# A hybrid decoder trunk on one core: tokens laid out feature by feature, the first norm's squares shared by two engines, router matrix and bias loaded in mid layer

## What is computed

```python
h = jnp.concatenate([meta, x], axis=1)           # 272 x 1024
for layer in range(2):
    u = rmsnorm(h, attn_norm[layer])             # h * rsqrt(mean(h*h) + eps) * gain
    ... = jnp.split(u @ w_in[layer], offsets)    # three token mixers and their gates
    h = h + mixed @ w_out[layer]
    u = rmsnorm(h, ffn_norm[layer])
    # layer 0: dense SwiGLU
    # layer 1: logits = u @ w_router + b_router, the best 2 of 8 experts of each token
return h[:, 16:]
```

## Time and profile before

| what | us |
|---|---|
| median of 3 runs (1881.51 to 1887.78) | 1884.59 |
| the profiled execution, its own time | 1884.42 |
| its span in the trace | 1882.5 |
| PE busy | 1815.8 (96%) |
| DVE busy | 1481.0 (79%) |
| ACT busy | 1284.6 (68%) |
| POOL busy | 111.2 (6%) |
| first product of the first job starts | 21.72 |
| PE idle ahead of the first router logits | 4.08 |

### The profile page before, as it was taken

One profiled execution on the slowest core, in us unless ns is written; L12 is line 12 of the kernel. 1 busy time (PEld: TensorE's weight loads), 2 busy tenths in 40 slices (PEclk: granted clock), 3 DMA queues, 4 the chain that ended last, 5 costly groups with the idle time before them and its releaser, 6 DMA issues.

```text
span 1882.5 us, 29560 instructions
## 1 busy us (share of the span) xinstructions
PE 1815.8 (96%) x10758; PEld 1583.2 (84%) x10758; DVE 1481.0 (79%) x1740; ACT 1284.6 (68%) x1633; POOL 111.2 (6%) x94
## 2 busy tenths in 40 slices
PE   7999999899998998998999999999999999999998
PEld 6988888899997888887888888888888888888886
DVE  5868787655547778777698898988989889898897
ACT  5777676433335776775577777777777777777776
POOL 0000003100010000004300000001000010000101
PEclk9999999999999999999999999999999999999999
DMA  5324324455454333334799999999999999999995
GB/s 196 125 91 133 102 101 141 135 173 177 163 176 149 121 103 112 122 102 152 266 410 370 389 371 371 404 366 391 379 359 406 368 387 369 373 405 369 362 407 214
DMA packets 87108, 485.37 MB, mean 258 GB/s; under 512 B 11630, under 2 KB 11934, under 8 KB 43744
## 3 DMA queue, kind: packets, MB, share of 16 engines
q1 hardware_dynamic: 84080, 476.14, 67.6%
q0 software_dynamic: 2944, 8.09, 1.7%
HBM read 477.17 MB, written 8.41 MB: 258 GB/s over the span
## 4 chain that ended last, share of the span: by engine, by line
PE 80%; DVE 10%; ACT 6%; issue 3%; DMA 1%; POOL 0%; SPq 0%; ACTq 0%; POOLq 0%; DVEq 0%
PE bank L1732 11%; PE bank L1733 11%; PE bank L1737 11%; PE bank L1439 8%; PE bank L1441 8%; PE bank L1440 7%; PE bank L1749 5%; PE bank L1750 5%; PE bank L1755 5%; DVE lo L949 2%; ACT hi L661 1%; PE bank L1764 1%; PE bank L1588 1%; PE bank L1608 1%; PE bank L1611 1%
## 5 line engine op out<-in xcount | busy, mean ns | idle before, releaser
L1271 DVE TENSOR_TENSOR mlo<-mraw,mhi 128x2048 fp32r<-128x2048 f32 x282 | 641.6, 2289 | 97.2 <-ACT mhi L842 84.5
L842 ACT ACTIVATE mhi<-mraw 128x2048 fp32r<-128x2048 f32 x283 | 540.7, 1916 | 110.7 <-PE bank L1755 49.8
L1439 PE MATMUL bank<-UH,hi 128*128 128x272 f32 (+1 forms) x1376 | 417.1, 303 | 18.7 <-DVE UL L962 8.6
L1441 PE MATMUL bank<-UH,lo 128*128 128x272 f32 (+1 forms) x1376 | 399.9, 291 | 0.0
L1440 PE MATMUL bank<-UL,hi 128*128 128x272 f32 (+1 forms) x1376 | 398.6, 290 | 0.0
L661 ACT ACTIVATE hi<-raw 128x1024 fp32r<-128x1024 f32 (+1 forms) x220 | 229.3, 1043 | 125.7 <-PE bank L1441 124.0
L1732 PE MATMUL bank<-mhi,xh 128*128 128x512 f32 x768 | 303.6, 395 | 0.4 <-DVE xl L1356 0.4
L1733 PE MATMUL bank<-mhi,xl 128*128 128x512 f32 x768 | 299.4, 390 | 0.0
L949 DVE TENSOR_TENSOR lo<-raw,hi 128x1024 fp32r<-128x1024 f32 (+1 forms) x220 | 266.2, 1223 | 41.6 <-ACT hi L661 41.1
L1439 PEld LDWEIGHTS bank<-UH,hi 128*128 128x128 f32 x1376 | 263.2, 191 | 32.1 <-issue 27.2
L1440 PEld LDWEIGHTS bank<-UL,hi 128*128 128x128 f32 x1376 | 264.5, 192 | 1.1 <-issue 0.5
(11 more groups left out here) (335 smaller groups left out, 2463.2 us busy)
## 6 DMA issues: line engine op xcount, KB each, us to landing
mraw<-in_w_exp SPq DMA_DIRECT2D x336, 1024.0 KB, 6.4
raw<-in_w_dense SPq DMA_DIRECT2D x212, 512.0 KB, 3.3
raw<-in_w_dense SPq DMA_DIRECT2D x8, 384.0 KB, 3.2
wuq<-in_w_uq SPq DMA_DIRECT2D x2, 1024.0 KB, 9.4
mixed<-in_x SPq DMA_DIRECT2D x2, 512.0 KB, 4.9
wukv<-in_w_ukv SPq DMA_DIRECT2D x2, 512.0 KB, 9.3
u_rows<-utok SPq DMA_DIRECT2D x1, 1024.0 KB, 4.4
y_rows<-acc SPq DMA_DIRECT2D x1, 1024.0 KB, 4.1
```

Of the source, the lines that this page charges most:

```text
L842: A_(mhi[k % MHI][:], mraw[k % MRAW][:], ACT.Copy).then_inc(mhi_made, 1)
L1271: TT(mlo[k % MRAW][:], mraw[k % MRAW][:], mhi[k % MHI][:].bitcast(F32), ALU.subtract).then_inc(mlo_made, 1)
L1439: MM(ps, h, xh_, start=first, stop=False)
L1441: return MM(ps, l, xh_, start=False, stop=last)
```

## The change

The host now hands the tokens over already joined with the meta tokens and laid out feature by feature (`tokens`, 128 x 8 x 272), so four DMAs of two feature tiles each fill `hT` directly; the transposes, the copies and the view `x_in` are gone. The identity and ones columns of the constants are loaded by a DMA that ACT issues. In the first norm ACT squares the even tiles, DVE the odd ones, and DVE adds each pair, so that PE sums four tiles. PE has "keep busy" matmuls on a tile of zeros: four ahead of the norm's sums, two behind them. Before the norm's `rr` only one `hi` and one `lo` are made; the others of the lookahead follow the norm. `wr` and `brb` get SBUF of their own, declared ahead of `guard`, are loaded in layer 1 ahead of job `r` 0, and have a semaphore of their own, `router_landed`; `MC` stays where it was. They take 256 and 32 bytes of each partition, so every tile declared between `guard` and `MC` lies 288 bytes further on than before (`mraw` 0 at byte 115104 and not 114816).

```diff
@@ -296,6 +296,8 @@
         eps = sb("eps", [P, 1])
+        wr = sb("wr", [P, KD, NE])
+        brb = sb("brb", [P, NE])
         guard = sb("guard", [P, 1])
@@ -307,8 +309,6 @@
         ident, ones = C[:, cc["ident"]], C[:, cc["ones"]]
-
-        x_in = mixed[:].rearrange("p k t -> p (k t)")[:, 0:2 * D].rearrange("p (b d) -> p b d", b=2)
@@ -387,8 +387,6 @@
         iota, tri, least = MC[:, 0:P], MC[:, P:2 * P], MC[:, 2 * P:2 * P + NE]
-        wr = sb("wr", [P, KD, NE])
-        brb = sb("brb", [P, NE])
         rt = sb("rt", [P, 14, 2, NE])
...
@@ -486,6 +485,10 @@
+        def squares_of_act(phase, m):
+
+            return KD * phase - KD // 2 + m + 1 if phase else m // 2 + 1
+
         need_u = {g: n for n, g in enumerate(g for g, (_, k, i) in enumerate(jobs)
@@ -494,15 +497,15 @@
-            sp.dma_start(vtok[0:META, 0:2, :], A["meta_tokens"].rearrange("t (k c) -> t k c", k=2)).then_inc(meta_landed, 16)
-            sp.dma_start(C[:, 0:2 * P], A["consts"][:, 0:2 * P]).then_inc(meta_landed, 16)
-            for half in range(2):
-                f = slice(half * (D // 2), (half + 1) * (D // 2))
-                sp.dma_start(x_in[:, :, f], A["x"][0, :, f].rearrange("(b p) d -> p b d", p=P)).then_inc(x_landed[half], 16)
+            for n in range(KD // 2):
+                sp.dma_start(hT[:, 2 * n:2 * n + 2, :], A["tokens"][:, 2 * n:2 * n + 2, :]).then_inc(x_landed[n], 16)
             sp.dma_start(par[:], A["params"]).then_inc(par_landed, 16)
             for g, (layer, kind, i) in enumerate(jobs):
                 if g == 2:
                     sp.dma_start(C[:, 2 * P:], A["consts"][:, 2 * P:]).then_inc(const_landed, 16)
+                if layer == DEPTH - 1 and kind == "r" and i == 0:
+                    sp.dma_start(wr[:], A["w_router"][0].rearrange("(k p) e -> p k e", p=P)).then_inc(router_landed, 16)
+                    sp.dma_start(brb[:], A["b_router"][0:1, :].broadcast_to([P, NE])).then_inc(router_landed, 16)
                 if kind == "gk" and i == 0:
@@ -521,8 +524,6 @@
             sp.dma_start(MC[:], A["moe_consts"]).then_inc(moe_const, 16)
-            sp.dma_start(wr[:], A["w_router"][0].rearrange("(k p) e -> p k e", p=P)).then_inc(moe_const, 16)
-            sp.dma_start(brb[:], A["b_router"][0:1, :].broadcast_to([P, NE])).then_inc(moe_const, 16)
...
@@ -663,7 +664,7 @@
                 if phase == 0:
-                    act.wait_ge(h_loaded, m + 1)
+                    act.wait_ge(x_landed[m // 2], 16)
                 else:
@@ -841,12 +842,14 @@
+            act.dma_start(C[:, 0:2 * P], A["consts"][:, 0:2 * P]).then_inc(ones_landed, 16)
             act.preload_act_table_set("natural_log_exp_and_others")
-            for m in range(KD):
+            for m in range(0, KD, 2):
                 square(0, m)
-            for g in range(LOOK):
+            split_hi(0)
+            norm(0)
+            for g in range(1, LOOK):
                 split_hi(g)
-            norm(0)
@@ -1235,17 +1238,22 @@
+            E.memset(ez[:], 0.0).then_inc(zero_made, 1)
             st(E.memset(guard[:], GUARD))
             E.memset(eps[:], EPS).then_inc(zeroed, 1)
             zero_pads()
-            for k in range(KD):
-                dve.wait_ge(x_turned, k + 1)
-                CP(hT[:, k, :], bank[2 + k % 2][:, 0:T]).then_inc(h_loaded, 1)
-            for g in range(LOOK_LO):
-                split_lo(g)
+            for m in range(1, KD, 2):
+                dve.wait_ge(x_landed[m // 2], 16)
+                st(TT(gt[:, m, :], hT[:, m, :], hT[:, m, :], ALU.mult))
+                dve.wait_ge(norm_sq, squares_of_act(0, m - 1))
+                st.wait()
+                TT(gt[:, m, :], gt[:, m, :], gt[:, m - 1, :], ALU.add).then_inc(pair_added, 1)
+            split_lo(0)
             gains = [par[:, l, PCOL[n]:PCOL[n] + 8] for l in range(2) for n in ("attn", "ffn")]
             dve.wait_ge(par_landed, 16)
             norm(0, gains[0])
+            for g in range(1, LOOK_LO):
+                split_lo(g)
@@ -1294,7 +1302,8 @@
                 expert_lo(k, k + 1)
-            dve.wait_ge(moe_const, 48)
+            dve.wait_ge(moe_const, 16)
+            dve.wait_ge(router_landed, 32)
             dve.wait_ge(norm_r, phase + 1)
@@ -1419,10 +1428,7 @@
-                for k in range(KD) if phase == 0 else (KD - 2, KD - 1):
-                    if phase == 0 and k == 0:
-
-                        pe.wait_ge(h_loaded, KD)
+                for k in range(1, KD, 2) if phase == 0 else (KD - 2, KD - 1):
                     ins = sum_squares(phase, k)
@@ -1430,8 +1436,11 @@
                     return MM(bank[2][:, 0:T], ones, gt[:, 0, :], start=True, stop=False)
-                pe.wait_ge(norm_sq, KD * phase + m + 1)
-                return MM(bank[2][:, 0:T], ones, gt[:, m, :], start=m == 0, stop=m == KD - 1)
+                if phase == 0:
+                    pe.wait_ge(pair_added, m // 2 + 1)
+                else:
+                    pe.wait_ge(norm_sq, squares_of_act(phase, m))
+                return MM(bank[2][:, 0:T], ones, gt[:, m, :], start=phase == 0 and m == 1, stop=m == KD - 1)
@@ -1618,19 +1627,17 @@
-            pe.wait_ge(meta_landed, 32)
-            for k in range(KD):
-                if k % 4 == 0:
-                    pe.wait_ge(x_landed[k // 4], 16)
-                if k >= 2:
-                    pe.wait_ge(h_loaded, k - 1)
-                b_ = bank[2 + k % 2]
-                TR(b_[:, 16:144], x_in[:, 0, k * P:(k + 1) * P], ident)
-                TR(b_[:, 144:272], x_in[:, 1, k * P:(k + 1) * P], ident)
-                TR(b_[:, 0:16], vtok[0:META, k // 4, (k % 4) * P:(k % 4 + 1) * P],
-                   ident[0:META, 0:META]).then_inc(x_turned, 1)
+            def keep_busy(n):
+
+                for _ in range(n):
+                    MM(bank[3][:, 0:T], ez[:, 0, 0:P], ez[:, 0, :], start=True, stop=True)
+
+            pe.wait_ge(zero_made, 1)
+            keep_busy(4)
+            pe.wait_ge(ones_landed, 16)
             pe.wait_ge(zeroed, 1)
             norm(0)
+            keep_busy(2)
@@ -1654,7 +1661,7 @@
                     if g == NG - 6:
-                        pe.wait_ge(moe_const, 48)
+                        pe.wait_ge(router_landed, 32)
                     logits(g - NG + 6)
...
@@ -1684,6 +1691,7 @@
             pe.wait_ge(chosen, 1)
+            pe.wait_ge(moe_const, 16)
             cs = rt[:, 6, :, :]
@@ -1811,7 +1819,9 @@
-    ins = {n: np.ascontiguousarray(a[n]) for n in WEIGHTS + ["x", "meta_tokens"]}
+    ins = {n: np.ascontiguousarray(a[n]) for n in WEIGHTS + []}
+    tokens = np.concatenate([np.asarray(a["meta_tokens"]), np.asarray(a["x"])[0]], 0)
+    ins["tokens"] = np.ascontiguousarray(tokens.T.reshape(KD, P, T).transpose(1, 0, 2))
     par = np.zeros((P, DEPTH, NPAR), np.float32)
```

More of the change, by code:

```diff
@@ L409, in bass_hybrid_trunk @@
         landed = [sem(f"landed{i}") for i in range(RAW)]
-        meta_landed, const_landed, par_landed, small_landed = (
-            sem("meta_landed"), sem("const_landed"), sem("par_landed"), sem("small_landed"))
-        x_landed = [sem(f"x_landed{i}") for i in range(2)]
+        x_landed = [sem(f"x_landed{i}") for i in range(KD // 2)]
+        zero_made, pair_added = sem("zero_made"), sem("pair_added")
+        ones_landed, const_landed, par_landed, small_landed = (
+            sem("ones_landed"), sem("const_landed"), sem("par_landed"), sem("small_landed"))
         small_used = sem("small_used")
@@ L429, in bass_hybrid_trunk @@
         mlanded = [sem(f"mlanded{i}") for i in range(MRAW)]
+        router_landed = sem("router_landed")
         moe_const, turned_u, turned_h = sem("moe_const"), sem("turned_u"), sem("turned_h")
@@ L571, in _ @@
                     phase, m = squares_at[g]
-                    pool.wait_ge(norm_sq, KD * phase + m + 1)
+                    pool.wait_ge(norm_sq, squares_of_act(phase, m))
                     if m > 1:
@@ L1665, in _ @@
                 logits(k)
-            pe.wait_ge(norm_sq, KD * phase + KD)
+            pe.wait_ge(norm_sq, squares_of_act(phase, KD - 1))
             for b in range(2):
```

1 line of the change is left out of this document (removed).

## The result

| | before | after |
|---|---|---|
| median of 4 runs, us | 1883.92 (1881.51 to 1887.78) | 1866.78 (1866.54 to 1867.47) |
| ratio, 95% interval | | 0.9905 (0.9892 to 0.9918) |
| profiled execution, its span | 1884.42, 1882.5 | 1866.54, 1864.8 |
| first product of job 0, job 1 | 21.72, 27.23 | 12.52, 18.67 |
| PE idle ahead of the first logits | 4.08 | none |

The account below looks back on a forecast made before the run. The prediction took PE's list of work, plus its waits and slow stretches, as the bound. 7.3 us at the start and 7.3 at the router, 14.6 off 1884.42, gave 1869.8 us, range 1865 to 1877.

Parts of the forecast that it names:

- The landing of the tokens and the sums: Start: last token pair lands at 7, is added at 8.0, and PE's sums end at about 8.8 (6.8 to 9.9).
- cost nothing: Start: the six zero products run beside other work; without that cover they would cost 1.4 to 2.7 us.
- The bound by `raw` 0: Start: `raw` 0 lands at 9.49, `hi` 0 ends at 10.55 ahead of `rr`; first product at 13.66, 8.06 gained.
- What goes back: Jobs 1 and 2: later `hi` and `lo` put job 1 at 19.83, job 2 at 22.95, leaving 7.3 us gained.
- `lo` 2 behind the `lb` values: Start: DVE makes `lo` 2 after the `lb` values, from 21.65 to 22.9, so job 2 starts at 22.95.
- The router: First logits: loading `wr` and `brb` earlier removes PE's wait and the low clock behind it, 7.3 us in all.
- The split into 4.24 of wait and 3.06 of clock: Logits: PE starts 4.24 us sooner without the wait, and full clock behind it saves 3.06 more.
- a rival only for the start: Start: the low clock falls on job 1 or 2 and takes 3.0 us back, 1872.8 us; chance 0.12.
- First expert chunk: Ahead of the expert loop: issued 1.1 us earlier, the chunk is there in time, by 0.9 us at worst.
- The sum: Whole kernel: 7.3 at the start plus 7.3 at the router, 14.6 off 1884.42, gives 1869.8 us.
- Only one gain: Start or router: only one gain comes through, 1876.0 if DMAs bind the loop or 1877.1; together chance 0.14.
- The 288 bytes: Moved tiles: new addresses slow PE, DVE or DMA; at 2.5% the loop is 23.8 us longer, 1893.6; chance 0.04.

Follow-up runs that it names:

- raw_later: The changed kernel with the rest of the constants (576 KB) issued ahead of `raw` 0 instead of behind `raw` 1; 1869.42 us, ratio 0.9928.
- router_only: The kernel before with only the router part: `wr` and `brb` in SBUF of their own, loaded in the middle of the second layer; 1877.56 us, ratio 0.9967.
- router_wait_filled: The kernel before with ten products of the constants ahead of PE's wait for `wr` and `brb`; 1884.64 us, ratio 1.0002.
- start_only: The changed kernel with `wr` and `brb` loaded at the old place, ahead of the first expert chunk; 1876.30 us, ratio 0.9959.
- changed_again: The changed kernel as it is, measured once more; 1867.34 us, ratio 0.9914, its profiled execution 1869.98 us.
- shifted_back: The changed kernel with 224 idle bytes behind `brb`, so tiles behind lie 512 bytes from their place in the kernel before; 1868.02 us, ratio 0.9914.

## Why the prediction was right, and where it was off

- **The landing of the tokens and the sums.** I took 7 for the landing of the last pair and 8.8 for the sums. The pair was there at 6.6, and the sums ended at 8.64 and decided nothing, as said. That the zero products "cost nothing" holds for the start. Whether the slower medians of the kernels without them are their doing is open; no step of mine had a term for it.
- **The bound by `raw` 0.** Right in kind: `hi` 0 ended directly ahead of `rr`, `lo` 0 directly ahead of `mixed`, and in raw_later the first product moved by just what `hi` 0 moved. The mis-sized step is "The bytes ahead of it are the same in both kernels (1245 KB and its own 512), and so is the number of issues", from which I took the landing at 9.49. It came at 8.44, 1.05 sooner. Equal bytes were not equal time, and a landing scatters by 0.9 here; the sum had no term for either, while the range did allow for "`raw` 0 landing 1 us sooner". The slow early DMA stretch of the kernel before (229 GB/s) would have warned me; I had not looked at it. First product 12.52 for 13.66.
- **What goes back.** Job 0 took 6.15 for the 6.17 of the forecast (19.83 - 13.66) and the wait for `lo` 1 was there. The last step, `lo` 2 behind the `lb` values, was no bound: job 2 did not wait. At job 2 8.5 were left for my 7.3: 1.05 is the landing, 0.1 the rest.
- **The router.** 7.29 in the trace for 7.3, and 7.30 in router_only. The split into 4.24 of wait and 3.06 of clock holds for these two executions, and router_wait_filled found the 3.04 behind the logits. But neither part is fixed: start_only lost 3.1 and 1.6 there and 2.27 in the routing, and router_wait_filled gave 2.01 back in the routing. I had reasoned "I take it that the clock stays up, since it fell only after this wait". That the clock can fall further on instead was a rival only for the start.
- **First expert chunk.** There 2.2 us ahead of its use; I had 0.9 as the worst case.
- **The sum.** 8.5 + 7.3 = 15.8 of the 17.7; the rest, 1.6 in the middle and 0.3 in the routing, is where the low clock fell in the two profiled executions. By the medians the gain is 17.1 the first time and 16.3 the second (1883.62 - 1867.34). The parts alone gave 7.8 and 6.6 us by their medians, 14.4 together; with intervals of some 2 to 3 us each this is no contradiction.
- **The rivals.** The clock did not take 3.0 us at job 1 or 2; it fell over job 0, from 12.7 to 16.1 us, where UL comes tile by tile. It can take 2.5 in the routing, as changed_again shows. "Only one gain" is out: both came, and the loop took 939.12 to 939.16 us in all fourteen traces. The 288 bytes are out by shifted_back.

## What to carry to other kernels

When two transfers carry the same bytes, look at the rate row of the microseconds in which they run before taking one's landing for the other's: here it was 229 against 401 GB/s. A term for the low clock is not a saving until the next places with short pauses have been looked at, since the clock may fall there instead, as it did in two traces. And two traces of a kernel that PE bounds should be cut at fixed instructions, with a second profiled execution of one of them, before 1 or 2 us are put down to the change.

## What was unexpected of the hardware

- The granted clock's column reads 1.00 up to its first fall, but PE's first products ran at half speed: eight records in 4.00 us from 1.61, and in the kernel before the records of the sums are 0.45 apart up to 16.21 and 0.23 from 16.57 on. The first clock record of the trace stands at 16.46 us in the kernel before and at 5.88 in the changed one, and ahead of it the column says nothing. The clock must be read from the spacing of products there.
- Which stretches run at 1.2 GHz differs between executions of one program: routing 19.76 or 22.31 us. Four of fourteen traces show the long form (22.0 and more), one of them of the changed kernel itself.
- Landings of the same tile behind the same transfers scatter by 0.9 us (`hi` 0, which waits for `raw` 0, starts at 8.02 to 8.96).
